# A two-block network on one core: the first half tile of attention's output weights split inside attention, the inputs of that projection split head by head, and small products around the barrier

## The chip, the cores and the metric

The kernel runs on one core of a Trainium2 chip. The metric is the device time of one execution in microseconds. The engines are TensorE (PE, with its weight loads as PEld), VectorE (DVE), ScalarE (ACT), GpSimd (POOL) and SyncE (SP, which here only issues DMAs).

## What is computed

Two networks of two layers each run one after the other on x of 256 tokens by 1024. The change lies in layer 0 of the first, windowed attention with a context of 256 further tokens, and its output projection with the residual and the layer norm:

```python
pz = h @ w_in
pzc = hc @ w_in
p, z = pz[..., :-E_WIDTH], pz[..., -E_WIDTH:]
pc, zc = pzc[..., :-E_WIDTH], pzc[..., -E_WIDTH:]
y, yc = attention_mixer(p, pc, attn_sink[j], row, col, not last)
x = layer_norm(alpha * x + gate * ((y * jax.nn.silu(z)) @ w_out[i]), ln_g[i], ln_b[i])
xc = layer_norm(alpha * xc + gate_c * ((yc * jax.nn.silu(zc)) @ w_out[i]), ln_g[i], ln_b[i])
```

Attention has 16 query heads of 128 (E_WIDTH is 2048) and 4 key heads; w_out[0] is 2048 x 1024. Layer 1 is an S5 mixer, and the second network has a gated-MLP and dilated attention layer, a gated linear attention layer and two convolutional feed-forward parts.

## The kernel before

**Phases.** The program is a row of phases: modulation, attention's input projection (qkvz), attention (`attention`, L807), its output projection (`residual_normalized`, L1033, with the names `out_...`), the S5 mixer (`ssm_...`), and so on. A phase is one block in which each engine has its own instruction list, written out by hand; semaphores order the engines against each other, and a barrier of all engines ends the block. Each engine reaches that barrier with a DRAIN, then POOL releases all. When more than 80 semaphores have been used up, a second barrier with a clearing of semaphores follows (L110, L111); this is so behind attention.

**Products in two parts.** The big products take f32 numbers as a sum of a lead and a rest: ACT copies a tile to the type fp32r (the lead), DVE subtracts the lead from the tile (the rest), and TensorE adds three products, lead by lead, lead by rest and rest by lead. `Split` (L215) does this for a weight that streams through a ring of two slots in SBUF (`core.ring`, 2 MB a slot). A weight tile of 1024 x 512 is split in two halves j = 0 and 1; `lead` (L266) and `rest` (L278) are one half, 128 partitions by 2048 elements, on ACT and on DVE. `start_scalar` (L287) and `start_vector` (L301) are the beginning of a phase: half 0, then the first piece of the other factor, then half 1, then its other pieces. With `src` given, as in the output projection, the other factor is split too, in pieces of four 128-row tiles (L299 the lead, L312 the rest). With `begun`, half 0 is taken as made before. `products` (L342) is TensorE's side: for each half it waits for the weights' rest and for the inputs' rest, and then goes through the token tiles t and the four rows k.

**Attention.** The loop runs `step(i)` for i from -1 to 17, on TensorE, ACT and DVE alike. In step i the scores of head i + 1, the turned outputs of head i - 2, the turned probabilities of head i, the turned queries of head i + 2 and the product with v of head i - 1 are made. The bank `ps_t` serves queries and outputs by turns. ACT's step is the copy to yzT (L964), the copy of the first probabilities (L968), the copy of the queries (L950) and the exponentials (L958, L959). DVE's step ends with the product of the output by z (L1016). POOL makes S5's input weights beside it, and SP carries them.

**Output projection.** n = 4 token tiles, two column groups of 512, and two ring tiles for each (the inner size is 2048). x is yzT, which holds one head in each of its 16 rows of tiles. POOL's work in this phase is `EarlyQuads` (L1487), ten pairs of small matrices for S5, six operations each (L1537, L1538, L1539), stored by SP (L1513); it begins when its tables (`ptab`, `cc`, L1506 and L1503) have landed and the first piece of x_rest is made:

```python
            def _(pool):
                pool.wait_ge(split.x_rest_made, 1)
                quads.make(pool)
```

SP's list issues the tables, the gate rows and the layer norm's rows, and the reloads of x and of the context first. The prefetch of S5's first weights stands before the last two pairs of POOL in SP's list. `spin(nc, bank, ident, n)` (L448) makes n products of ident by itself into a bank that nobody reads; 20 of them (L1077) stand at the end of this phase's TensorE list, and each product in the code is two records in the trace (L451 x40 for 20).

**Memory.** z, kn, q and v lie at the right end of SBUF (`within(heads, ...)`, L3478 on) and are given back behind attention.

Of the kernel before, what the change touches and what calls it, by code (L numbers as in the profile page):

```python
# [14 lines left out]
F32 = mybir.dt.float32  # L15
# [199 lines left out]
class Split:  # L215
# [6 lines left out]
    def __init__(self, core, ph, groups, halves, ntt, mm_done, src=None, lhs=None, slots=None, begun=False, flip=0):  # L222
        self.flip = flip
# [5 lines left out]
        if src is not None:  # L229
            lhs = [part("x_lead", [P, halves * KT, ntt * P]), part("x_rest", [P, halves * KT, ntt * P])]  # L230
# [53 lines left out]

    def _x_pieces(self):
        return range(2 * self.halves) if self.src is not None else ()

    def start_scalar(self, act, norm=None):

        for piece in range(2 * self.halves):  # L290
# [58 lines left out]
    def products(self, pe, bank, free, part_wait=None, between=None, unrolled=False, soon=None, after=None):  # L349
        nc, last_half = self.core.nc, 2 * self.halves - 1  # L350

        def group(g, parity):
            for sem, n in free:
                pe.wait_ge(sem, g * n + 1)
            for half in range(2 * self.halves):
                j = half % 2
                pe.wait_ge(self.rest_made, g * (2 * self.halves) + half + 1)
                if self.src is not None:
                    pe.wait_ge(self.x_rest_made, half + 1)
                for t in range(self.ntt):  # L360
                    for k in range(HK):
                        if part_wait is not None and t == 0 and g == 0:
# [24 lines left out]
class EarlyHalf:  # L387
# [419 lines left out]
def attention(core, q, kn, v, z, kT, work, yzT, xc):  # L807
# [7 lines left out]
    with phase(core, "attn") as ph:  # L815
# [22 lines left out]
        spare = ph.sb("spare", [P, DM])  # L838
        weights = InputWeights(core, ph, W_QKVZ, NWB - W_QKVZ, [core.x[:, s // 2, s % 2 * NW:(s % 2 + 1) * NW] for s in range(4)], [xc[:, s // 2, s % 2 * NW:(s % 2 + 1) * NW] for s in range(4)], [spare[:, s * NW:(s + 1) * NW] for s in range(2)])
# [5 lines left out]
        with ph.block() as block:  # L845
# [13 lines left out]
            def _(pe):  # L859
# [73 lines left out]
                for i in range(-1, NH + 2):  # L933
                    step(i, i % 2)

            @block.scalar
            def _(act):
# [37 lines left out]
                for i in range(-1, NH + 2):  # L975
                    step(i, i % 2)

# [2628 lines left out]
```

## Time and profile before

| | before |
|---|---|
| median of 3 runs (lowest to highest) | 1646.36 us (1642.62 to 1649.51) |
| the profiled execution: its time / its span | 1644.76 us / 1643.0 us |
| mean granted TensorE clock | 0.972 |
| PE / DVE / ACT / POOL busy | 94% / 60% / 48% / 40% |
| attention's last product to the first of out | 442.4 to 451.6 us |
| first product of out to S5's first | 451.6 to 546.4 us |

Times of rows are microseconds from the span's start. "Busy" of TensorE is modelled from the issue of its matmuls. The granted clock is a share of 2.4 GHz; 0.5 is 1.2 GHz.

### The profile page before, as it was taken

How to read it: one execution, taken by the hardware profiler on the slowest of the kernel's cores; microseconds unless marked ns; L12 is line 12 of the kernel's file. 1: busy time of each engine (PE TensorE's matmuls, PEld its weight loads, DVE VectorE, ACT ScalarE, POOL GpSimd, SP SyncE). 2: the span in 40 equal slices, each digit the busy share in tenths (PEclk: the TensorE clock that was granted, in tenths of full speed). 3: DMA queues.
4: the chain of work that ended last, by engine and by line, in shares of the span. 5: the costliest groups of instructions: out<-in, count | busy, mean ns of one | idle time of the engine just before them, and what ended most of it. 6: DMA issues, size and time to landing. Idle time of an engine off the chain costs nothing. (4 is left out here: it accounts for less than half of the span.)

```text
span 1643.0 us, 28520 instructions
## 1 busy us (share of the span) xinstructions
PE 1539.9 (94%) x11502; PEld 1321.2 (80%) x11502; DVE 981.9 (60%) x1349; ACT 794.7 (48%) x1075; POOL 649.5 (40%) x497
## 2 busy tenths in 40 slices
PE   4799999799699899999999999989999999999998
PEld 0488888588688688888889987778999877789997
DVE  6157722288654538757837546745766565557675
ACT  2532122355521576787564435645455364564552
POOL 0068989599699791749502106111000100210000
PEclk8899999999999999999989999989999999999999
DMA  9976877566452687988976455415453342264441
GB/s 387 426 265 213 273 239 249 167 194 193 149 207 95 218 253 207 258 250 259 231 244 236 167 189 198 154 52 210 182 224 153 132 157 111 103 231 184 201 163 42
DMA packets 120300, 331.32 MB, mean 202 GB/s; under 512 B 33509, under 2 KB 73189, under 8 KB 103929
## 3 DMA queue, kind: packets, MB, share of 16 engines
q1 hardware_dynamic: 117318, 304.20, 53.7%
q10 hardware_dynamic: 2868, 25.54, 4.3%
q8 instruction: 80, 1.31, 0.3%
q14 instruction: 34, 0.27, 0.1%
HBM read 283.48 MB, written 37.83 MB: 196 GB/s over the span
## 5 line engine op out<-in xcount | busy, mean ns | idle before, releaser
L3312 PE MATMUL ffn_ps<-ffn_x_lead,w_lead 128*128 128x256 f32 x672 | 188.4, 280 | 1.1 <-DVE w_rest L3391 1.1
L3312 PE MATMUL ffn_ps<-ffn_x_lead,w_rest 128*128 128x256 f32 x672 | 188.6, 281 | 0.0
L3312 PE MATMUL ffn_ps<-ffn_x_rest,w_lead 128*128 128x256 f32 x672 | 188.4, 280 | 0.0
L401 POOL TENSOR_TENSOR w_rest<-resident_ring,w_lead 128x2048 fp32r<-128x2048 f32 x7 | 32.1, 4590 | 387.9 <-ACT w_lead L397 200.3
L3391 DVE TENSOR_TENSOR w_rest<-resident_ring,w_lead 128x2048 fp32r<-128x2048 f32 x42 | 96.1, 2292 | 83.8 <-ACT w_lead L3356 83.8
L365 PE MATMUL qkvz_ps<-qkvz_w_lead,h_lead 128*128 128x512 f32 x320 | 125.8, 393 | 2.6 <-POOL h_rest L683 2.6
L3312 PEld LDWEIGHTS ffn_ps<-ffn_x_lead,w_lead 128*128 128x128 f32 x672 | 126.1, 188 | 2.1 <-issue 1.4
L3312 PEld LDWEIGHTS ffn_ps<-ffn_x_rest,w_lead 128*128 128x128 f32 x672 | 126.4, 188 | 0.7
L3312 PEld LDWEIGHTS ffn_ps<-ffn_x_lead,w_rest 128*128 128x128 f32 x672 | 126.3, 188 | 0.0
L365 PE MATMUL qkvz_ps<-qkvz_w_rest,h_lead 128*128 128x512 f32 x320 | 125.4, 392 | 0.0
L365 PE MATMUL qkvz_ps<-qkvz_w_lead,h_rest 128*128 128x512 f32 x320 | 125.2, 391 | 0.0
L282 DVE TENSOR_TENSOR w_rest<-resident_ring,w_lead 128x2048 fp32r<-128x2048 f32 x33 | 78.1, 2369 | 64.0 <-ACT w_lead L276 63.7
L276 ACT ACTIVATE qkvz_w_lead<-resident_ring 128x2048 fp32r<-128x2048 f32 x20 | 38.5, 1924 | 147.3 <-PE qkvz_ps L365 136.3
L282 DVE TENSOR_TENSOR qkvz_w_rest<-resident_ring,qkvz_w_lead 128x2048 fp32r<-128x2048 f32 x20 | 56.0, 2798 | 88.7 <-ACT qkvz_w_lead L276 88.7
L3356 ACT ACTIVATE w_lead<-resident_ring 128x2048 fp32r<-128x2048 f32 x42 | 80.1, 1912 | 50.7 <-PE ffn_ps L3312 50.6
L276 ACT ACTIVATE w_lead<-resident_ring 128x2048 fp32r<-128x2048 f32 x33 | 63.2, 1915 | 79.6 <-PE odd_ps L365 26.0
L1884 PE MATMUL ssm_ps_u<-h_lead,w_lead 128*128 128x512 f32 (+1 forms) x256 | 91.0, 355 | 6.8 <-DVE w_rest L2168 2.1
L1481 POOL TENSOR_TENSOR resident_x<-xc,resident_x 128x512 f32<-128x512 f32 x64 | 92.9, 1452 | 5.0
L2168 DVE TENSOR_TENSOR w_rest<-resident_ring,w_lead 128x1024 fp32r<-128x1024 f32 x32 | 48.9, 1530 | 68.8 <-ACT w_lead L2019 68.4
L1884 PE MATMUL ssm_ps_u<-h_lead,w_rest 128*128 128x512 f32 (+1 forms) x256 | 87.6, 342 | 1.4 <-issue 1.4
L1884 PE MATMUL ssm_ps_u<-h_rest,w_lead 128*128 128x512 f32 (+1 forms) x256 | 87.3, 341 | 0.0
L2318 PE MATMUL glu_ps<-h_lead,w_lead 128*128 128x256 f32 x256 | 71.7, 280 | 2.8 <-DVE w_rest L2358 1.5
(566 smaller groups left out, 4460.1 us busy)
## 6 DMA issues: line engine op xcount, KB each, us to landing
resident_ring<-in_ffn_gu SPq DMA_DIRECT2D x22, 2048.0 KB, 9.1
ffn_wd<-in_ffn_down SPq DMA_DIRECT2D x22, 1024.0 KB, 4.9
resident_ring<-in_ada_w SPq DMA_DIRECT2D x8, 2048.0 KB, 12.8
xc<-s_q_scratch SPq DMA_DIRECT2D x128, 128.0 KB, 3.3
resident_x<-in_s_bT SPq DMA_DIRECT2D x64, 256.0 KB, 3.8
resident_ring<-in_attn_w_in ACTq DMA_DIRECT2D x8, 2048.0 KB, 10.9
s_W_scratch<-resident_x SPq DMA_DIRECT2D x64, 256.0 KB, 2.7
resident_ring<-in_s_w SPq DMA_DIRECT2D x32, 512.0 KB, 6.0
```

Source lines behind the costliest of these rows:

```text
L276: self.core.nc.scalar.activation(self.w[0][j], self.core.tile(r)[:, j * HK:(j + 1) * HK, :], ACT.Copy).then_inc(self.lead_made, 1)
L282: self.core.nc.vector.tensor_tensor(self.w[1][j], self.core.tile(r)[:, j * HK:(j + 1) * HK, :], self.w[0][j].bitcast(F32), ALU.subtract).t ...
L365: last = nc.tensor.matmul(bank(parity, t), self.lhs[x][:, half * HK + k, t * P:(t + 1) * P], self.w[w][j][:, k, :], start=(half, k, x, w) ...
L401: self.core.nc.gpsimd.tensor_tensor(self.slots[1][0], self._raw(r), self.slots[0][0].bitcast(F32), ALU.subtract).then_inc(self.rest_made, 1)
L1481: g.tensor_tensor(b, q(0), b, ALU.mult).then_inc(self.scaled, 1)
L1884: last = nc.tensor.matmul(out, w[:, s, k, :], hparts[x][:, k, cols], start=k == 0 and x == 0 and w is w_lead, stop=k == KT - 1 and w is w_ ...
L2168: v.tensor_tensor(w_rest[:, u % 2], raw, w_lead[:, u % 2].bitcast(F32), ALU.subtract).then_inc(rest_made, 1)
L2318: last = nc.tensor.matmul(ps[s][:], w[s][:, k, :], parts[x][:, k, :], start=k == 0 and x == 0 and w is w_lead, stop=k == ET - 1 and w is w ...
L3312: last = nc.tensor.matmul(ps[s][f][:, m, :], w_part[w][m][:, k, f * P:(f + 1) * P], x_part[x][:, k, :], start=(k, w, x) == (0, 0, 0), stop ...
L3356: nc.scalar.activation(w_part[0][m], raw(s, m), ACT.Copy).then_inc(w_lead_made, 1)
L3391: v.tensor_tensor(w_part[1][m], raw(s, m), w_part[0][m].bitcast(F32), ALU.subtract).then_inc(w_rest_made, 1)
```

## The change

1. Half 0 of the first output weight tile is split inside attention: `EarlyHalf` takes the lead on ACT behind step 8 and the rest on DVE behind step 15. The parts lie where q lies (`w_parts`), in columns of heads that are done; the lead of yzT lies where z lies, kn takes the gate rows.
2. The first four heads of yzT are split one at a time (`fine_x`), and TensorE waits for each of them in its first token tile alone. POOL waits for four counts of `x_rest_made` in place of one, which now is the same four heads.
3. Small products: 12 at the end of attention's TensorE list, 10 at the start of the output projection's.

```diff
+    def x_parts_of(self, piece):
+        if self.fine_x and piece == 0:
+            return [(slice(k, k + 1), k + 1) for k in range(HK)]
+        return [(slice(piece * HK, (piece + 1) * HK), piece + (HK if self.fine_x else 1))]
...
             if self.src is not None:
-                ks = slice(piece * HK, (piece + 1) * HK)
-                self.core.nc.scalar.activation(self.lhs[0][:, ks], self.src[:, ks], ACT.Copy).then_inc(self.x_lead_made, 1)
+                for ks, count in self.x_parts_of(piece):
+                    self.core.nc.scalar.activation(self.lhs[0][:, ks], self.src[:, ks], ACT.Copy).then_inc(self.x_lead_made, 1)
...
             if self.src is not None:
-                ks = slice(piece * HK, (piece + 1) * HK)
-                dve.wait_ge(self.x_lead_made, piece + 1)
-                self.core.nc.vector.tensor_tensor(self.lhs[1][:, ks], self.src[:, ks], self.lhs[0][:, ks].bitcast(F32), ALU.subtract).then_inc(self.x_rest_made, 1)
+                for ks, count in self.x_parts_of(piece):
+                    dve.wait_ge(self.x_lead_made, count)
+                    self.core.nc.vector.tensor_tensor(self.lhs[1][:, ks], self.src[:, ks], self.lhs[0][:, ks].bitcast(F32), ALU.subtract).then_inc(self.x_rest_made, 1)
...
             for half in range(2 * self.halves):
                 j = half % 2
+                fine = self.fine_x and (g, half) == (0, 0)
                 pe.wait_ge(self.rest_made, g * (2 * self.halves) + half + 1)
-                if self.src is not None:
-                    pe.wait_ge(self.x_rest_made, half + 1)
+                if self.src is not None and not fine:
+                    pe.wait_ge(self.x_rest_made, self.x_parts_of(half)[-1][1])
                 for t in range(self.ntt):
                     for k in range(HK):
+                        if fine and t == 0:
+                            pe.wait_ge(self.x_rest_made, k + 1)
...
-    def rest(self, pool, r):
-        pool.wait_ge(self.lead_made, 1)
-        self.core.nc.gpsimd.tensor_tensor(self.slots[1][0], self._raw(r), self.slots[0][0].bitcast(F32), ALU.subtract).then_inc(self.rest_made, 1)
+    def rest(self, eng, r, ops=None):
+        eng.wait_ge(self.lead_made, 1)
+        (ops or self.core.nc.gpsimd).tensor_tensor(self.slots[1][0], self._raw(r), self.slots[0][0].bitcast(F32), ALU.subtract).then_inc(self.rest_made, 1)
...
+        following = EarlyHalf(core, ph, [[m] for m in first_weights])
+        FOLLOWING_AT = 8
...
                 for i in range(-1, NH + 2):
                     step(i, i % 2)
+                spin(nc, ps_s[0], ident, 12)
...
                 for i in range(-1, NH + 2):
                     step(i, i % 2)
+                    if i == FOLLOWING_AT:
+                        act.wait_ge(core.landed[0], 16 * (core.used[0] + 1))
+                        following.lead(act, 0)
...
                 for i in range(-1, NH + 2):
                     step(i, i % 2)
+                    if i == NH - 1:
+                        following.rest(dve, 0, nc.vector)
...
-        split = Split(core, ph, 2, 2, n, mm_done, src=yzT)
+        x_rest = ph.sb("x_rest", [P, ET, n * P], F32R)
+        split = Split(core, ph, 2, 2, n, mm_done, src=yzT, lhs=[x_lead, x_rest], slots=slots, begun=True, fine_x=True)
...
             def _(pool):
-                pool.wait_ge(split.x_rest_made, 1)
+                pool.wait_ge(split.x_rest_made, HK)
                 quads.make(pool)
...
             def _(pe):
+                spin(nc, ps[1][0], core.ident, 10)
                 split.products(pe, lambda s, t: ps[s][t][:], [])
...
+                    x_lead = nc.alloc_sbuf_tensor_at("out0_x_lead", [P, ET, NTOK], F32R, offset=nc.sbuf_top)
...
+                    w_parts = nc.alloc_sbuf_tensor_at("out0_w", [P, HK, 4, NW], F32R, offset=nc.sbuf_top)
+                    slots = [[w_parts[:, :, 2 * j + i, :] for j in range(2)] for i in range(2)]
...
-                                        again=((core.x[:], rows_of(d["x"])), (xc[:], rows_of(d["ctx"]))))
+                                        again=((core.x[:], rows_of(d["x"])), (xc[:], rows_of(d["ctx"]))),
+                                        x_lead=x_lead, slots=slots, gate=kn[:].rearrange("p t n -> p (t n)").rearrange("p (r n) -> p r n", r=2))
```

TensorE's list around the end of attention, before (the two branches are the end of one phase and the start of the next, with the barrier between them; names in square brackets are semaphores, called by the first owner of their number):

```order
L912 MATMUL attn_ps_t<-resident_ident,attn_yz 128x128 [waits attn_qT_ready,attn_yzT_ready,attn_yz_ready]
L912 MATMUL attn_ps_t<-resident_ident,attn_yz 128x128 x3
L845 UNCONDITIONAL_BRANCH
L1073 UNCONDITIONAL_BRANCH [waits barrier_Pool_Activation_PE_DVE_SP_release]
L365 MATMUL out_ps<-out_w_lead,out_x_lead 128x512 [waits ada_modT_done,ada_kept0]
```

and with the change:

```order
L923 MATMUL attn_ps_t<-resident_ident,attn_yz 128x128 [waits attn_qT_ready,attn_yzT_ready,attn_yz_ready]
L923 MATMUL attn_ps_t<-resident_ident,attn_yz 128x128 x3
L460 MATMUL attn_ps_s<-resident_ident 128x128 x12
L856 UNCONDITIONAL_BRANCH
L1090 UNCONDITIONAL_BRANCH [waits barrier_Pool_Activation_PE_DVE_SP_release]
L460 MATMUL out_ps<-resident_ident 128x128 x10
L374 MATMUL out_ps<-out_w,out_x_lead 128x512 [waits ada_modT_done,ada_kept0]
```

Twelve small products now stand ahead of the barrier and ten behind it; the first real product still waits for a weight rest and an input rest.

DVE's list at the same place, before:

```order
L1016 SCALAR_TENSOR_TENSOR attn_yz<-attn_ps_y,attn_rden,z 128x128 [waits attn_yz_turned,attn_pv_ready]
L845 UNCONDITIONAL_BRANCH
L1095 UNCONDITIONAL_BRANCH [waits barrier_Pool_Activation_PE_DVE_SP_release]
L282 TENSOR_TENSOR out_w_rest<-resident_ring,out_w_lead 128x2048 [waits ada_bias_made]
L312 TENSOR_TENSOR out_x_rest<-yzT,out_x_lead 128x2048 [waits ada_kept1]
```

and with the change:

```order
L410 TENSOR_TENSOR out_w<-resident_ring,out_w 128x4x512 [waits attn_early_lead_made]
L1031 SCALAR_TENSOR_TENSOR attn_yz<-attn_ps_y,attn_rden,z 128x128 [waits attn_yz_turned,attn_pv_ready]
L856 UNCONDITIONAL_BRANCH
L1113 UNCONDITIONAL_BRANCH [waits barrier_Pool_Activation_PE_DVE_SP_release]
L318 TENSOR_TENSOR out_x_rest<-yzT,out_x_lead 128x512 [waits ada_kept1] x4
L282 TENSOR_TENSOR out_w<-resident_ring,out_w 128x4x512 [waits ada_bias_made]
L318 TENSOR_TENSOR out_x_rest<-yzT,out_x_lead 128x2048 [waits ada_kept1] x3
```

The subtraction of half 0 moved ahead of the last product with z, and the first input piece became four. POOL's and SP's lists keep their order.

## Rows read from the trace of the kernel before

**Rows 1.** The page: busy time, share of the span and instructions of each engine.
```profile
PE 1539.9 (94%) x11502; PEld 1321.2 (80%) x11502; DVE 981.9 (60%) x1349; ACT 794.7 (48%) x1075; POOL 649.5 (40%) x497
```
**Rows 2.** Windows: us, busy (x) of PE, PEld, DVE, ACT, POOL; clock, DMA share, GB/s.
```profile
443.00:452.00 9.00, 0.46 (x2) 0.42 (x2) 5.03 (x3) 7.57 (x5) 0.46 (x1) 0.58 0.57 193
452.00:455.00 3.00, 3.00 (x9) 2.33 (x9) 3.00 (x2) 3.00 (x3) 3.00 (x2) 0.55 1.03 399
455.00:540.00 85.00, 85.00 (x377) 70.36 (x376) 41.77 (x39) 15.56 (x11) 82.10 (x56) 1.00 0.43 161
...
546.30:550.00 3.70, 3.03 (x24) 2.59 (x24) 2.13 (x3) 2.97 (x6) 1.31 (x2) 1.00 0.83 268
550.00:553.40 3.40, 2.49 (x13) 1.86 (x14) 3.31 (x7) 3.40 (x9) 1.16 (x2) 1.00 0.95 310
```
**Rows 3.** Timeline of TensorE: start, duration, what, count [idle before <-releaser].
```profile
442.41 0.66 PE L912 MATMUL attn_ps_t<-resident_ident,attn_yz 128*128 128x128 f32 x4 [1.22 <-DVE attn_yz L1016]
451.61 0.77 PE L365 MATMUL out_ps<-out_w_lead,out_x_lead 128*128 128x512 f32 x1 [8.54 <-DVE out_x_rest L312]
...
454.71 0.39 PE L365 MATMUL out_ps<-out_w_rest,out_x_lead 128*128 128x512 f32 x1
```
**Rows 4.** Timeline of DVE and ACT around the barrier.
```profile
441.23 1.13 DVE L1016 SCALAR_TENSOR_TENSOR attn_yz<-attn_ps_y,attn_rden,z 128x128 f32<-128x128 f32 x4 [3.43 <-PE attn_ps_y L903]
...
445.03 1.91 ACT L276 ACTIVATE out_w_lead<-resident_ring 128x2048 fp32r<-128x2048 f32 x1 [1.33 <-PEq L111]
...
449.18 2.28 DVE L312 TENSOR_TENSOR out_x_rest<-yzT,out_x_lead 128x2048 fp32r<-128x2048 f32 x1
451.38 2.28 DVE L282 TENSOR_TENSOR out_w_rest<-resident_ring,out_w_lead 128x2048 fp32r<-128x2048 f32 x1
```
**Rows 5.** Timeline of POOL in out, and its window over the phase.
```profile
451.54 3.10 POOL L1537 TENSOR_TENSOR out_vp_v<-out_vp_ptab,out_vp_cc 128x512 f32<-128x512 f32 x1 [14.68 <-DVE out_x_rest L312]
454.60 3.15 POOL L1538 TENSOR_TENSOR out_vp_tmp<-out_vp_ptab,out_vp_cc 128x512 f32<-128x512 f32 x1
...
481.46 1.11 POOL L1537 TENSOR_TENSOR out_vp_v<-out_vp_ptab,out_vp_cc 128x512 f32<-128x512 f32 x1
...
542.42 1.27 POOL L1539 TENSOR_TENSOR out_vp_v<-out_vp_v,out_vp_tmp 128x512 f32<-128x512 f32 x1
451.50:543.70 92.20, 89.09 (x60) 0.98 0.47 176
```
**Rows 6.** SP's issue of cc; DMA issues (KB, us to landing), 425:545, then 444.9:450.
```profile
445.38 0.90 SPq L1503 DMA_DIRECT2D out_vp_cc<-in_s_cA  x2
...
s_V_scratch<-out_vp_v SPq DMA_DIRECT2D x20, 256.0 KB, 2.2
...
out_vp_cc<-in_s_cA SPq DMA_DIRECT2D x2, 128.0 KB, 4.5
```
**Rows 7.** The barrier lines L845 and L1051: duration ns, start; and the small products.
```profile
L845 PEldq DRAIN  x1: 700/700/700, 442.4 to 442.4; - x1
L845 ACTq DRAIN  x1: 627/627/627, 443.1 to 443.1; - x1
L1051 PEldq DRAIN  x1: 2173/2173/2173, 542.7 to 542.7; - x1
L1051 ACTq DRAIN  x1: 1907/1907/1907, 543.6 to 543.6; - x1
L1051 SPq DRAIN  x1: 7/7/7, 546.1 to 546.1; - x1
540.19 4.63 PE L451 MATMUL out_ps<-resident_ident 128*128 128x128 f32 x40
```
**Rows 8.** Timeline of ACT and TensorE at the change from step 8 to 9.
```profile
388.72 0.60 ACT L964 ACTIVATE yzT<-attn_ps_t 128x512 f32<-128x512 f32 x1 [1.02 <-PE attn_ps_t L912]
389.83 0.60 PE L871 MATMUL attn_ps_t<-resident_ident,q 128*128 128x128 f32 x4
```
**Rows 9.** One line of DVE in S5's start: a subtraction of 128x512.
```profile
L673 DVE TENSOR_TENSOR h_rest<-ssm_ps_s,h_lead x2: 690/690/691, 551.1 to 555.7; 128x512 fp32r<-128x512 f32 x2
```

More of the change, by code:

```diff
@@ L215, with __init__ @@
 class Split:
-    def __init__(self, core, ph, groups, halves, ntt, mm_done, src=None, lhs=None, slots=None, begun=False, flip=0):
-        self.flip = flip
+    def __init__(self, core, ph, groups, halves, ntt, mm_done, src=None, lhs=None, slots=None, begun=False, flip=0, fine_x=False):
+        self.flip, self.fine_x = flip, fine_x
         self.core, self.groups, self.halves, self.ntt, self.mm_done, self.src = core, groups, halves, ntt, mm_done, src
@@ L228, in __init__ @@
         self.w, self.begun = slots, begun
-        if src is not None:
+        if src is not None and lhs is None:
             lhs = [part("x_lead", [P, halves * KT, ntt * P]), part("x_rest", [P, halves * KT, ntt * P])]
@@ L804, in _, with attention @@
                     dve.sem_inc(dve_free, LT)
-def attention(core, q, kn, v, z, kT, work, yzT, xc):
+def attention(core, q, kn, v, z, kT, work, yzT, xc, first_weights):
     nc, d = core.nc, core.d
@@ L1030, in residual_rows, with residual_normalized @@
     return 16 * (len(rows) + len(more))
-def residual_normalized(core, name, weights, xs, yzT, following, again):
+def residual_normalized(core, name, weights, xs, yzT, following, again, x_lead, slots, gate):
     nc, d = core.nc, core.d
@@ L1038, in residual_normalized @@
     with phase(core, name) as ph:
-        gate = ph.sb("gate", [P, 2, DM])
         ln_g, ln_b = ph.sb("ln_g", [P, KT]), ph.sb("ln_b", [P, KT])
@@ L3458, in build @@
                 context = [(xc[:, t, :], 1) for t in range(LT)]
-                with ExitStack() as heads, ExitStack() as outputs:
+                with ExitStack() as heads, ExitStack() as values, ExitStack() as outputs:
                     z = within(heads, "z", [P, TT, E], side="right")
+                    x_lead = nc.alloc_sbuf_tensor_at("out0_x_lead", [P, ET, NTOK], F32R, offset=nc.sbuf_top)
                     kn = within(heads, "kn", [P, TT, KVW], side="right")
@@ L3464, in build @@
                     q = within(heads, "q", [P, TT, E], side="right")
-                    v = within(heads, "v", [P, TT, KVW], side="right")
+                    w_parts = nc.alloc_sbuf_tensor_at("out0_w", [P, HK, 4, NW], F32R, offset=nc.sbuf_top)
+                    slots = [[w_parts[:, :, 2 * j + i, :] for j in range(2)] for i in range(2)]
+                    v = within(values, "v", [P, TT, KVW], side="right")
                     with ExitStack() as inner:
@@ L3471, in build @@
                         kT, work = within(inner, "kT", [P, KVH, NTOK]), within(inner, "work", [P, KT - 1, NTOK])
-                        attention(core, q, kn, v, z, kT, work, yzT, xc)
-                    heads.close()
+                        attention(core, q, kn, v, z, kT, work, yzT, xc, [of[0] for of in slots])
+                    values.close()
                     rows_of = lambda m: m.rearrange("(t p) n -> p t n", p=P)
                     residual_normalized(core, "out0", "w_out0", latent + context, yzT, lambda sp: s5_prefetch(core, sp),
-                                        again=((core.x[:], rows_of(d["x"])), (xc[:], rows_of(d["ctx"]))))
+                                        again=((core.x[:], rows_of(d["x"])), (xc[:], rows_of(d["ctx"]))),
+                                        x_lead=x_lead, slots=slots, gate=kn[:].rearrange("p t n -> p (t n)").rearrange("p (r n) -> p r n", r=2))
                 wparts = [within(ctx, n, [P, HK * NW], F32R, side="right") for n in ("w0_lead", "w0_rest")]
```

## Prediction

> **What bounds the kernel now.** I read the page first. TensorE is busy 94% of the span [rows 1], so the question is where it is not busy or not fast, and which of those places this change touches. The chain that ended last reaches back only to the last feed-forward part, far behind the edit, so it says nothing here. The windows by stage do [rows 2]: from 443 to 452 us TensorE does 0.46 us of work at a mean granted clock of 0.58. After that, from 455 to 540, it is busy all the time at 1.00. The hole lies between attention and the output projection ("out"). The timeline of TensorE shows both sides [rows 3]: its last transposes of attention start at 442.41, the first product of out at 451.61. The products that start from 451.61 to 454.71 are seven in 3.10 us; at the later pace, 377 products in 85.0 us [rows 2], or 0.226 us each, they would take 1.6. So the low clock (1.2 GHz, fallen while TensorE idled) costs 1.5 us, and the wait itself 8.5.
>
> What fills the wait is in the rows of ACT and DVE [rows 4]: after the barrier ACT copies half a weight tile (1.91 us from 445.03) and then a piece of yzT. DVE subtracts after each, and its first piece of x_rest ends at 449.18 + 2.28 = 451.46, when TensorE starts.
>
> The same semaphore starts POOL, and the end of the phase has to be read from there. POOL makes S5's matrices from 451.54 and ends its last operation at 542.42 + 1.27 = 543.69, with no pause to speak of: sixty operations in 92 us [rows 5]. SP stores the last one (landing 2.2 us after issue in the median [rows 6]) and reaches the closing barrier at 546.1 [rows 7]. ACT is there at 543.6 + 1.91 = 545.5, TensorE at 542.7 + 2.17 = 544.8. **The phase ends when POOL's chain and its last store do**; TensorE's own path has 0.6 us of slack already. A gain ahead of the products counts only as far as POOL starts earlier too.
>
> **The change, part by part.**
>
> *Half tile split inside attention.* ACT gets 1.91 us [rows 4] behind the exponentials of step 8. The ACT queue is idle 1.02 us there before the copy to yzT at 388.72 [rows 8]; that copy starts about 0.8 late and ends at 390.1, and TensorE's transposes of q, at 389.83 now, need its bank. TensorE never pauses in these steps, so about +0.3 us stays. DVE's 2.28 us goes ahead of its last product with z, at 441.23, before which it idles 3.43 us [rows 4]: free. If that cover were gone, attention's end would move by what sticks out of it. POOL, which such a subtraction holds up (below), has ended its attention work by then (idle 14.68 us before 451.54, so from 436.9 [rows 5]).
>
> *Twelve small products before the barrier.* Forty records of the same 128x128 product take 4.63 us behind out [rows 7], 0.116 each, and each one in the code is two records. Twelve are 2.8 us, from 442.85 to 445.65. Does the barrier wait for them? The drain of TensorE's queue at the end of out begins at 542.7 and takes 2.17 us, to 544.8, exactly where those 40 records end, and in attention it ends with the last transposes (442.4 + 0.70) [rows 7]. So it does wait. ACT's drain, the last one now, ends at 443.1 + 0.63 = 443.7 [rows 7]. The barrier moves from there to 445.7, **+2.0 us**, with SP, DVE, POOL and ACT held behind it. The Trainium skill (Perfetto Trace Analysis, section "Per-engine timelines", on sequencer-only instructions such as DRAIN) draws a DRAIN with only the sequencer and the semaphore in it; by that the small products would not hold the barrier and this term would be 0. The 2.17 us row speaks against it, and the row decides.
>
> Out then starts at 445.03 + 0.3 + 2.0 = 447.3.
>
> *Ten small products behind the barrier, inputs head by head.* The ten take 20 x 0.116 = 2.3 us: to 449.6. The first head needs one ACT copy of 128x512 (0.60 [rows 8]) and one DVE subtraction of that shape (0.69 [rows 9]): 448.6, so the small products, not the data, set the start. Later heads come every 0.6 to 0.7 us, and TensorE uses three products (0.68) for each. The second half of the tile follows 10.9 us later, its parts are made by about 456: covered. With TensorE busy on both sides of a gap of some 1.5 us I take the clock as staying at 2.4 GHz, since in the window from 546.3 it is 1.00 behind such a gap [rows 2]. TensorE gains 451.6 - 449.6 = 2.0 plus the 1.5: **3.5 us**; its last product ends near 536.7, ACT's last normalization near 542.0.
>
> *POOL.* It waits for four heads (447.3 + 0.6 + 4 x 0.65 = 450.5) but also for its tables: the first DMA for cc is issued at 445.38, 0.4 us into the phase, and lands 4.5 us later [rows 6], so at 452.2. Before, they were 1.7 us ahead of need; now they are last. What does 0.7 us of lateness cost? While DVE subtracts in SBUF, a POOL operation of 1.11 us takes 3.10 or 3.15 [rows 5]: the first one starts at 451.54, DVE's subtraction from 451.38 ends at 453.66, and POOL ends at 454.64. With the change ACT has four short copies (2.0) and one lead (1.9) before that subtraction: it starts at 451.3 again and ends at 453.6, and POOL's first operation, though later, ends near 454.6 as before. So **0** for POOL's chain, with 546.3 as the phase's end again. The Trainium skill (SBUF — State Buffer, section "Who interferes with whom") says that the one which starts first holds the pair for the whole instruction, and that the other blocks. Were it a sharing of bandwidth, the phase would end 0.7 later. The trace agrees with the first.
>
> Bounds of this term: if the barrier is not held, the second weight subtraction and with it POOL come 2.0 earlier: -2.0. If the lateness counts in full: +0.7.
>
> *What is late next.* TensorE ends its 20 small products at 541.3 and then idles 5 us instead of 1.6. No row has an idle time of that length: 1.6 us leaves the clock at 1.00, 8.5 lets it fall [rows 2]. I take it as falling. In rows 3 it cost 1.5 us, and S5's start has 0.7 us of idle time in its first 3.7 us [rows 2] that takes up some: **+0.9**. Bounds: 0, and with all of 546.3 to 553.4 at half clock 5.5 us of busy time more, less 1.6 idle: +3.9.
>
> The other edits cost nothing: the gate rows land in kn instead of a tile of their own, the same two DMAs; the weight parts are strided by 4 x 512 over 2048 elements, the same element count.
>
> Sum: +0.9 on the profiled execution's own 1644.76, so 1645.7. That execution is 1.6 us under the median of the three runs (1646.36); 0.9 on the median gives 1647.3. I say **1646.5 us**. Differences under 0.5% (8.2 us) can't be told from none in this kernel.
>
> **The rivals.**
>
> *Faster, the barrier is not held or POOL does start earlier.* For it: the barrier's own wait is short, and the small products write banks that nobody waits for. Against it: the 2.17 us drain. POOL's end moves by -2.0, and S5's start costs less: 1646.5 - 2.0 - 0.9, near 1643.6. Chance 0.17. Were POOL no bound at all, the 3.5 and the 2.0 would both arrive: 1641. Chance 0.03.
>
> *Slower, the clock at S5's start.* One mechanism: the longer idle time before 546.4. It decides if the clock is still at 1.2 GHz once S5's first transposes are over and its products begin. Price up to +3.9 in place of 0.9: 1649.5, and 1650.5 with the 0.7. For it: every part of 3.5 us gained before is idle time there. Against it: the start is full of waits for ACT and POOL. The Trainium skill (TensorE: Matmul & The Clock Gate, Part 1) calls the throttled state the default that activity releases; that is this case. Chance 0.15.
>
> *The change does not do what it says:* the gaps of 1.2 us between attention's last products are enough for the clock to fall at 444 as now [rows 2, 3]; then the small products run at half pace, the barrier comes another 1.2 later, POOL's chain with it: 1647.7. Chance 0.08.
>
> **How the numbers follow.** The forecast has 0.57. No case reaches 8.2 us: the best is 5.5 under the forecast, the worst 4 over. The three runs of one kernel lie within 6.9 us, though, and such scatter puts a few per cent on either side: faster by over 0.5% 0.04, within 0.5% 0.91, slower 0.05. The range, 1642 to 1650.5, holds the forecast with its scatter and nearly all of two rivals, and leaves out the last 0.03.
>
> **What would show it.** Right: TensorE's drain ends attention near 445.7 and the phase starts near 447.3; ten small products at 1.00, first product near 449.6; POOL's first operation near 452 and long; POOL's end near 543.7, S5 near 546.4 with a clock under 1. Wrong: a phase start near 445.4, POOL's last operation before 542, or an S5 that starts at full clock after a shorter gap.

## The result, and the profile after

| | before | changed |
|---|---|---|
| median, side by side on one chip | 1644.11 us (20 runs, 1638.9 to 1650.6) | 1652.29 us (20 runs, 1645.47 to 1656.48) |
| ratio, 95% interval | | 1.005 (1.0038 to 1.0062) |
| profiled execution, span | 1643.0 us | 1654.3 us |

The ratio is that of the fast runs and need not be the quotient of the two medians; with its interval it decides here and below.

The changed kernel is 8.2 us slower. The forecast was 1646.5 us in a range up to 1650.5, so the result lies outside the range, on the slower side.

First the place that the prediction was about. The barrier behind attention in the changed kernel: duration of the drains in ns and their start.
```profile
L856 ACTq DRAIN  x1: 626/626/626, 444.2 to 444.2; - x1
L856 PEldq DRAIN  x1: 2173/2173/2173, 444.7 to 444.7; - x1
L856 SPq EVENT_SEMAPHORE  x1: 17/17/17, 447.0 to 447.0; - x1
```
TensorE's drain takes 2.17 us where it took 0.70 [rows 7] and ends at 446.8, when the small products do. ACT's ended at 444.8. So the small products hold the barrier by 2.0 us, the size predicted. Then the timeline of TensorE, POOL and the windows of the phase:
```profile
443.97 2.84 PE L460 MATMUL attn_ps_s<-resident_ident 128*128 128x128 f32 x24
448.16 2.47 PE L460 MATMUL out_ps<-resident_ident 128*128 128x128 f32 x20 [1.35 <-PEq L111]
450.39 0.72 PE L374 MATMUL out_ps<-out_w,out_x_lead 128*128 128x512 f32 x2
```
```profile
453.71 1.81 POOL L1555 TENSOR_TENSOR out_vp_v<-out_vp_ptab,out_vp_cc 128x512 f32<-128x512 f32 x1 [16.61 <-DMA out_vp_cc<-in_s_cA]
...
543.56 1.27 POOL L1557 TENSOR_TENSOR out_vp_v<-out_vp_v,out_vp_tmp 128x512 f32<-128x512 f32 x1
```
```profile
443.00:452.00 9.00, 7.17 (x55) 6.75 (x56) 2.92 (x6) 4.39 (x6) 0.00 (x0) 1.00 0.31 96
...
547.10:550.50 3.40, 2.26 (x11) 2.29 (x12) 1.13 (x3) 1.16 (x2) 0.58 (x1) 0.57 0.48 193
```
The clock stays at 1.00 across the barrier (0.58 in [rows 2]), the first product of out starts 2.3 us after the phase does, POOL waits for the cc transfer, and the clock is low when S5 starts. All that was foreseen. The phase of out ends at 548.1, against 546.3 before: 1.8 us late.

The loss is behind it. I compare the lengths of the phases, each from one release of the barrier to the next in the two traces. The span grew by 11.3 us, 3.1 us more than the medians: the profiled execution of the changed kernel (1656.04 us) is 3.8 us above its median, that of before (1644.76) 0.7. **S5 +11.05** (301.55 to 312.60), attention +3.39 (138.85 to 142.24), output projection -1.27 (101.35 to 100.08), modulation +1.00, input projection -1.28, S5's gate +0.57, the dilated attention layer of the second network -1.94, all the others together -0.2. The change edits nothing in S5. Windows over exactly S5, before and changed (length, busy us of PE, PEld, DVE, ACT, POOL, then clock, DMA share, GB/s):
```profile
546.30:847.90 301.60, 283.84 (x4028) 250.98 (x4028) 191.20 (x297) 211.54 (x298) 178.11 (x138) 0.95 0.81 232
```
```profile
548.10:860.80 312.70, 290.96 (x4028) 256.33 (x4028) 190.58 (x297) 210.68 (x298) 178.28 (x138) 0.93 0.78 222
```
The same 4028 products, on an engine that is busy 7.1 us longer (the clock is low more of the time, 42.9 us in place of 27.3) and idle 4.0 us longer. What TensorE's idle time in S5 ended with, of the kind that no semaphore explains ("issue"), before and then changed:
```profile
PE ssm_ps_u L1884 <- issue: 2.6, 2, 1.4
PE ssm_ps_y L1937 <- issue: 0.9, 1, 0.9
```
```profile
PE ssm_ps_y L1955 <- issue: 6.7, 4, 2.0
PE ssm_ps_s L2006 <- issue: 1.8, 1, 1.8
PE ssm_ps_u L1902 <- issue: 1.5, 2, 1.2
PE ssm_ps_l L1937 <- issue: 1.1, 1, 1.1
```
3.5 us have become 11.1. One pause of 1.18 us near 570 is in every kernel below; without it 2.3 have become 9.9, in two pauses before and seven now. Such a pause looks like this in the timeline, and beside it stands the DMA of the 1.1 us from 666.8:
```profile
669.23 0.31 PE L1955 MATMUL ssm_ps_y<-ssm_V,ssm_hs 128*32 128x128 f32 x3 [1.89 <-issue]
```
```profile
q1 hardware_dynamic: 108, 0.18, 44.0%
q8 instruction: 1, 0.02, 5.4%
```
A packet on the queue "instruction" ran from 666.90 to 667.86, and TensorE went on 1.4 us after its end. Each of the nine pauses ends 1.3 to 1.6 us after the end of such a packet (the one near 570 doesn't: 14 and 25 us). The page of the changed kernel says how large these are:
```profile
q8 instruction: 80, 1.31, 0.3%
```
80 packets, 1.31 MB: 16 KB each. PE's compiled list has 20,592 instructions before, and 80 packets of 256 instructions make 20,480, so that a packet brings about 256 of them. The Trainium skill has the same number (Advanced Engine Details and Errata, section "ISA Cache": a line is 16 KB or 256 instructions). The trace agrees.

The change adds 22 small products, each of four instructions of TensorE: 88. (The page of before counts 28,520 instructions, that of the kernel with these products alone, spins_only below, 28,608.) Everything behind them lies 88 places later in the list, and so the point at which a new packet is needed falls on another product of S5.

**Theory A**: where the packets' borders fall in S5 costs the time; the change merely shifts them. **Theory B**: the change's own work (spins, drain, clock) leaves S5 slower. "Place" below is by how many instructions of TensorE S5 stands later than before. A small product is called a spin.

### The profile page after: what moved, and what is told of

Read it like the earlier page. It is cut to its first block and busy times, and to the rows that moved or that the text cites. A ratio compares the mean times of both kernels' runs of the same rounds, so it can differ in the third digit from the quotient of the medians.

```text
span 1654.3 us, 28616 instructions
## 1 busy us (share of the span) xinstructions
PE 1556.6 (94%) x11546; PEld 1332.0 (81%) x11546; DVE 982.2 (59%) x1352; ACT 794.4 (48%) x1078; POOL 646.0 (39%) x497
## 3 DMA queue, kind: packets, MB, share of 16 engines
q8 instruction: 80, 1.31, 0.3%
## 5 line engine op out<-in xcount | busy, mean ns | idle before, releaser
L1499 POOL TENSOR_TENSOR resident_x<-xc,resident_x 128x512 f32<-128x512 f32 x64 | 87.1, 1362 | 5.0
L374 PE MATMUL out_ps<-out_w,out_x_lead 128*128 128x512 f32 x256 | 80.3, 395 | 0.0
## 6 DMA issues: line engine op xcount, KB each, us to landing
resident_ring<-in_attn_w_in ACTq DMA_DIRECT2D x8, 2048.0 KB, 10.2
```

Source lines behind the costliest of these rows:

```text
L374: last = nc.tensor.matmul(bank(parity, t), self.lhs[x][:, half * HK + k, t * P:(t + 1) * P], self.w[w][j][:, k, :], start=(half, k, x, w) ...
L1499: g.tensor_tensor(b, q(0), b, ALU.mult).then_inc(self.scaled, 1)
```

## The experiments

### First four: the place alone, and the change without its small products

pad88 and pad128 are the kernel before with an unused semaphore's increments at the head of TensorE's list, after_pad168 is the changed kernel with such increments (88 + 168 = 256), and no_spins is the changed kernel with the early half tile and the fine inputs but no spins (place 0).

```diff
 # pad88, at the start of the modulation's list of TensorE (128, 168 in the others)
+                for _ in range(88):
+                    pe.sem_inc(pad, 1)
```
```diff
 # no_spins
-                spin(nc, ps_s[0], ident, 12)
...
-                spin(nc, ps[1][0], core.ident, 10)
```

> The kernel before with nothing of the change, but 88 semaphore increments on TensorE's list at the very start of the program, where TensorE idles until 10.7 us. They make TensorE's list exactly as much longer as the change does (20680 instructions in place of 20592), so every later instruction of TensorE stands where it stands with the change. Theory A (the S5 phase got slower because TensorE's instructions arrive later at some places, which depends on where they stand in the list): barrier to barrier S5 takes 306 to 313 us in place of 301.6, with pauses of TensorE of 1 to 2 us that no semaphore explains, and the time is 4 to 9 us over the kernel before. Theory B (S5 got slower because it starts after a longer idle time, at a low clock and with shifted transfers): nothing changes, S5 within 2 us of 301.6 and the time within 1.5 us.

> The kernel before with 128 semaphore increments at the start of TensorE's list, half a fetch. Theory A: S5 differs from 301.6 by some microseconds, either way, by where the boundaries of the fetches fall; I expect +2 to +9. Theory B: no change, within 1.5 us.

> The changed kernel with 168 semaphore increments at the start of TensorE's list: with the change's 88 they make 256 instructions, the size of one fetch of TensorE's instructions (16 KB, 64 bytes each), so that each later instruction stands at the same place within a fetch as before the change. Theory A: S5 takes 301 to 304 us, and the time is 1 to 3 us over the kernel before (attention +3.4, out -1.3 as in the changed kernel's trace). Theory B: S5 stays at 306 to 313 us and the time at +8.

> The changed kernel without its 12 and 10 small products; the split inside attention and the head-by-head inputs stay. TensorE's list is as long as before the change (20592). The barrier is no longer held by TensorE. Theory A: S5 within 2 us of 301.6, attention's phase 139 to 140.5 (from 138.9), out's first product about 2 us behind the phase's start, at 1.2 GHz; POOL's chain starts 1 to 2 us earlier than before the change; time between -3 and 0 against the kernel before. Theory B: the idle time before S5 is still there (TensorE's path is ahead of POOL's by more than before), so S5 is 4 to 9 us longer and the time +3 to +7.

Measured, against 1643.18 us of before in the same comparison: pad88 1655.03 (ratio 1.0061, 1.0041 to 1.008), pad128 1653.2 (1.005, 1.0032 to 1.0068), after_pad168 1651.58 (1.0045, 1.0029 to 1.006), no_spins 1641.4 (0.9984, 0.9969 to 0.9998). S5 took 312.51, 308.45, 298.36 and 301.52 us. Each length of a phase, here and below, is that of one profiled execution. Window and waits of S5 in pad88:
```profile
550.10:862.60 312.50, 292.56 (x4028) 258.74 (x4028) 189.05 (x297) 211.19 (x298) 178.04 (x138) 0.93 0.78 223
```
```profile
PE ssm_ps_y L1940 <- issue: 3.8, 3, 2.3
PE ssm_ps_u L1887 <- issue: 3.3, 2, 2.1
PE ssm_ps_s L1991 <- issue: 2.0, 1, 2.0
```
88 instructions that compute nothing make S5 of the kernel *before* 11 us longer, as in the changed one (312.60). Its total is above what I expected (+10.0 us by the ratio, against +4 to +9). By its total, after_pad168 is a miss for theory A (+7.4 against +1 to +3), but its S5 is back and shorter than expected (301 to 304); the modulation took 84.72 us in place of 74.48, since the increments stand in front of TensorE's first product. That 10.2 us is the padding's own price. It also mixes into pad88 (2.5 us) and pad128 (4.0), so the padding had to be hidden. Both figures are rough, since in the seven kernels of this study without padding in the modulation it takes 74.3 to 76.8 us.

### Padding where TensorE waits anyway, and the parts of the change

TensorE waits 23.8 us for weights in the modulation, over 8 waits. The padding goes in front of the waits behind the first one, which alone takes 10.7 us; 13.1 us are left to hide it in.

```diff
 # spread88 (before, 11 each), after_spread168 (changed, 21 each), spread256 (before, 32 each)
                 def unit(g):
+                    if 1 <= g <= 8:
+                        for _ in range(11):
+                            pe.sem_inc(pad, 1)
```
```diff
 # spins_only: the kernel before, with
+                spin(nc, ps_s[0], ident, 12)
...
+                spin(nc, ps[1][0], core.ident, 10)
```
```diff
 # late_spins: the changed kernel, without
-                spin(nc, ps_s[0], ident, 12)
```

> The kernel before plus 88 increments of an unused semaphore in PE's list, 11 in front of each of the weight waits of units 1 to 8 of the modulation, where PE waits for DMA anyway (23.8 us over 8 waits). It is pad88 without the price of the increments. Theory A (where PE's later instructions lie, modulo 256 of the 64-byte instructions that one fetch brings, sets how often PE stands without a wait in S5): the modulation stays at 74.5 to 75.5 us (pad88: 76.99), S5 takes 309 to 314 us as in pad88 (312.51) and in the changed kernel (312.60), total +8 to +11 us. Theory P (pad88's loss was the price of its own increments): S5 stays at 301.5, total within +-2 us.

> The changed kernel plus 168 increments of an unused semaphore, 21 in front of each of the weight waits of units 1 to 8 of the modulation. With the change's 88 PE instructions, PE's list behind them stands 256 instructions later than before, so its fetch boundaries fall where they fell. Theory A: the modulation takes 75 to 77 us (after_pad168: 84.72, the increments in front of the first wait cost it 10), S5 takes 298 to 303 us (changed kernel 312.60, after_pad168 298.36), attention stays at +3.4 us, the output projection at -1.3 to -2, total 1643 to 1646 us, 0 to +2 against before. Theory B (the spins and the drain themselves leave S5 slower): S5 stays at 309 to 313 and the total at +8.

> The kernel before with the two rows of spins alone, 12 in front of the barrier behind attention and 10 behind it; no early half tile, no fine inputs. Theory A with the drain: PE's drain at attention's end waits for the spins, attention +2 to +3 us; the 10 spins stand beside the 8.5 us in which PE waits for the first inputs, output projection 101 to 101.5; S5 309 to 314; total +10 to +13 us. Theory B' (the early half, not the spins, costs attention its 3.4 us): attention within 0.5 us of before, total +8 to +10.

> The changed kernel without the 12 spins in front of the barrier (48 PE instructions fewer, so its list stands 40 instructions later than before, not 88); the 10 spins behind the barrier stay. Drain theory: attention falls from 142.2 us to 139.2 to 140.2 (no_spins 139.23), ACT or POOL end the barrier again; the output projection takes 99.5 to 100.5. Theory A: S5 takes another length, that of a place between 0 (301.5) and 88 (312.5): 300 to 313 us. Total 1640 to 1650 us. Rival: the 12 spins cost nothing in front of the barrier and attention stays at 142.

Measured, before 1642.95: spread88 1653.53 (1.0061, 1.004 to 1.0082), **after_spread168 1641.8 (0.9996, 0.9981 to 1.0012)**, spins_only 1650.88 (1.0043, 1.0026 to 1.006), late_spins 1642.7 (1.0006, 0.999 to 1.0023). The changed kernel with 168 idle instructions more is as fast as before: its loss of 8.2 us is gone, though all spins, the held barrier and the early half tile are still in it. That is a little better than expected (0 to +2 us, S5 298 to 303). spread88 comes out as theory A has it, but for 0.5 us more in the modulation (76.03). The S5 of spread88, the term alone, and then that of after_spread168, each with its pauses:
```profile
548.60:859.40 310.80, 290.68 (x4028) 256.44 (x4028) 190.04 (x297) 211.13 (x298) 178.21 (x138) 0.93 0.78 225
```
```profile
PE ssm_ps_y L1941 <- issue: 3.5, 3, 2.0
PE ssm_ps_u L1888 <- issue: 2.8, 2, 1.6
PE ssm_ps_s L1992 <- issue: 1.1, 1, 1.1
PE ssm_ps_l L1923 <- issue: 0.5, 1, 0.5
```
```profile
546.90:843.40 296.50, 282.12 (x4028) 249.33 (x4028) 190.31 (x297) 211.74 (x298) 178.26 (x138) 0.96 0.82 236
```
```profile
PE ssm_ps_y L1959 <- issue: 1.5, 1, 1.5
PE ssm_ps_u L1906 <- issue: 1.4, 2, 1.2
PE ssm_ps_s L1978 <- issue: 1.2, 1, 1.2
```
Theory B falls. Late_spins' S5, at place 40, took 299.22 us (just below the 300 to 313 expected), so that not every shift costs. spins_only has the long S5 (309.59), but its total is +7.1 us where I expected +10 to +13: its S5 is 8.0 us longer, at the lower end of what I expected. The drain comes out as predicted: attention takes +2.2 us with the spins alone (141.02) and +0.4 with the early half alone (139.29 in late_spins, 139.23 in no_spins). The barrier in spins_only and in late_spins:
```profile
L845 ACTq DRAIN  x1: 626/626/626, 443.5 to 443.5; - x1
L845 PEldq DRAIN  x1: 2173/2173/2173, 444.0 to 444.0; - x1
```
```profile
L856 PEldq DRAIN  x1: 700/700/700, 444.3 to 444.3; - x1
L856 ACTq DRAIN  x1: 627/627/627, 445.0 to 445.0; - x1
```

### Is it the number, or the number modulo 256? Does it need S5 behind it?

```diff
 # behind88: the kernel before, in S5's gate phase, right behind S5
             @block.tensor
             def _(pe):
+                for _ in range(88):
+                    pe.sem_inc(pad, 1)
```
```diff
 # no_spins_no_fine, on no_spins
-        split = Split(core, ph, 2, 2, n, mm_done, src=yzT, lhs=[x_lead, x_rest], slots=slots, begun=True, fine_x=True)
+        split = Split(core, ph, 2, 2, n, mm_done, src=yzT, lhs=[x_lead, x_rest], slots=slots, begun=True)
...
-                pool.wait_ge(split.x_rest_made, HK)
+                pool.wait_ge(split.x_rest_made, 1)
```
no_spins_spread256 is no_spins with the 8 x 32 increments.

> The kernel before plus 256 increments of an unused semaphore, 32 in front of each of the weight waits of units 1 to 8 of the modulation: nearly three times the increments of spread88 (+10.6 us), but a whole fetch block of 256 instructions. Theory A (place modulo 256): S5 as before or as in after_spread168, 296 to 302 us, the increments cost the modulation 0 to 3 us, total -3 to +2 us. Theory N (more instructions in PE's list, whatever their number, cost S5 time): S5 309 or more, total at least +10 us.

> The kernel before plus 88 increments of an unused semaphore at the start of PE's list in the phase behind S5 (the gate). It is the control of spread88: the same number of instructions, but S5 stands in front of them. Theory A: S5 stays at 301.5 us, the gate phase takes 0 to 2.5 us more for the increments, the phases behind it move by less than 1 us each, total 0 to +4 us. Theory N (any 88 more instructions in PE's list, wherever they stand): total +8 us or more.

> The changed kernel without its 22 spins (early half tile and fine inputs stay), plus 256 increments spread over units 1 to 8 of the modulation. It is the version that the runs so far point to: no_spins gave 0.9984, and the two kernels that stand 256 instructions later had the shortest S5 (298.36 and 296.40 us against 301.5 at 0). If that gain is of the place (an absolute place, not only modulo 256), S5 takes 296 to 299 us and the total is 1636 to 1640 us; if the place counts modulo 256 alone and those two were scatter, S5 takes 301 to 302 and the total is that of no_spins, 1640 to 1643 us.

> no_spins with the first inputs in one piece again instead of head by head: what is left of the change is the early half tile. PE's first product comes when the whole first piece is subtracted, about 2.5 us later after the phase's start than in no_spins (1.65 us). If the output projection ends with POOL's chain and the landing of its last transfer (in no_spins SP's wait ends 544.65, ACT's drain 543.55, a slack of 1.1 to 1.4 us), the phase takes 99.8 to 101.2 us (no_spins 99.80, before 101.35), total 0 to +1.5 us over no_spins, 1641 to 1643. Rival: each microsecond of PE's start counts, phase 102 or more.

Measured, before 1642.04: spread256 1646.06 (1.0025, 1.001 to 1.0041), behind88 1657.32 (1.0098, 1.0078 to 1.0119), no_spins_spread256 1646.49 (1.0027, 1.0012 to 1.0042), no_spins_no_fine 1641.31 (1.0005, 0.9993 to 1.0016).

With 256 instructions S5 takes 298.93 us, with 88 it took 310.83: not the number, the place. (The unused semaphore is in both, so it isn't that either. The pages of all five kernels at place 256 count 81 packets of 16 KB, those of the others 80.) The total of spread256 still missed what I expected by 2 us, since the modulation took 80.10 (+5.6 us). behind88 shows why. S5 in front of its padding is as before (300.36 us), which is theory A's part; but the gate phase took 110.52 us in place of 95.44, and its waits and the increments read:
```profile
PE glu_ps L2321 <- issue: 14.8, 1, 14.8
```
```profile
L2310 PEldq EVENT_SEMAPHORE  x88: 51/51/51, 850.7 to 864.0; - x88
```
88 increments in 13.3 us are 0.15 us each, five times what I had worked out from pad88 (2.5 us / 88). There most of the increments lay beside the first wait: TensorE's first product starts at 14.40 us in pad88 and at 10.69 in before. The total of behind88, +16 us, meets what its expectation wrote down for theory N (+8 or more) and misses theory A's 0 to +4. But 15.1 us of it lie in the gate phase, where the increments stand, and S5 is not longer: it is the padding's price, and no evidence for N.

no_spins_spread256 paid 8.0 us in the modulation (82.32, no_spins 74.29) and had an S5 of 298.99, 2.5 us shorter; the total had to miss what I expected by the price of the padding. In no_spins_no_fine the first product comes 4.5 us after the phase's start (1.65 in no_spins) and the output projection takes 101.73 us in place of 99.80. Its barrier:
```profile
L1067 ACTq DRAIN  x1: 1906/1906/1906, 547.1 to 547.1; - x1
L1067 SPq DRAIN  x1: 7/7/7, 547.6 to 547.6; - x1
```
ACT ends it, at 549.0, 1.4 us after SP: TensorE's own path, which ACT's last normalization follows, is the last again. TensorE's last product starts 96.0 us after the phase's start, against 92.8 in no_spins. So the fine inputs earn about 1.9 us of the phase in these profiles, more than the 1.5 us I took as the upper end. In the totals the two can't be told apart for certain: 1.0005 and 0.9984, with intervals that overlap.

### Two candidates, padded with products

So far the size of the place's effect was mixed with the price of the increments. Two last kernels pad no_spins with spins.
```diff
 # no_spins_spun64 (8 in front of units 1 to 8; no_spins_spun10: 2 in front of units 1 to 5)
                         pe.wait_ge(kept_done[g % 2], g // 2)
+                    if 1 <= g <= 8:
+                        spin(nc, ps[g % 2], core.ident, 8)
```

> no_spins plus 64 products of the unit matrix with itself in the modulation, 8 in front of each of the weight waits of units 1 to 8: 256 PE instructions, a whole fetch block, by products in place of semaphore increments. 64 products take 64 x 0.12 to 0.23 us = 7.4 to 15 us, beside 24 us of waits for weights. Theory A: S5 takes 296 to 301 us as in the four kernels that stand 256 later (298.36, 296.40, 298.93, 299.00), the modulation 74.3 to 77, total 1637 to 1642 us. Rival (a price of the modulation, a falling S5 only by increments): total 1643 or more.

> no_spins plus 10 products of the unit matrix in the modulation, 2 in front of the weight waits of units 1 to 5: PE's list stands 40 instructions later than in no_spins, the place of late_spins, whose S5 took 299.22 us. Theory A: S5 298 to 301 us, the modulation 74.3 to 76, total 1638 to 1642 us. Rival (the place says nothing, late_spins' S5 was scatter): S5 301.5, total that of no_spins, 1640 to 1643.

Measured, before 1642.71: no_spins_spun64 1640.13 (0.9984, 0.9971 to 0.9997), no_spins_spun10 1641.71 (0.9999, 0.9984 to 1.0014). S5 300.46 and 296.16 us. Padding with products acts like padding with increments, and is cheap (modulation 75.8 and 76.3 us). The S5 of no_spins_spun10 is below what I expected (298 to 301), yet its total doesn't differ for certain from that of no_spins. no_spins_spun64 and no_spins, both 0.16% under before, are the fastest kernels of the study; both beat the changed kernel clearly and before only barely. Neither shows a gain over no_spins in the total. S5 by place, over all profiled executions (the column of pauses leaves out the one near 570):

| place | kernels | S5, us | pauses behind a packet, sum, us | at the low clock, us |
|---|---|---|---|---|
| 0 | before, no_spins, no_spins_no_fine, behind88 | 300.4 to 301.6 | 2.3 to 3.9 | 27.3 to 30.7 |
| 40 | late_spins, no_spins_spun10 | 299.2, 296.2 | 3.1, 1.7 | 23.9, 20.5 |
| 88 | changed, pad88, spread88, spins_only | 309.6 to 312.6 | 6.8 to 9.9 | 37.5 to 46.3 |
| 128 | pad128 | 308.5 | 9.7 | 27.3 |
| 256 | after_pad168, after_spread168, spread256, no_spins_spread256, no_spins_spun64 | 296.4 to 300.5 | 2.5 to 5.3 | 20.5 to 26.4 |

In all five kernels at 88 and 128 S5 takes at least 6.9 us longer than in any of the eleven others and has more of these pauses, whatever else is in them. The smaller differences, of places 40 and 256 against 0, are not shown by the totals: late_spins and no_spins_spun10 have 1.0006 and 0.9999, no_spins with its longer S5 has 0.9984.

## Why the prediction was wrong

*Where it failed.* The sum priced each edit at the place where it stands and ended with "no case reaches 8.2 us". It counted the 22 spins as 2.8 and 2.3 us of TensorE, and not as 88 instructions in front of everything that follows. The trace of before had the sign of it, in the two pauses shown above that end with no semaphore, and no rival asked what they were. The missing term is +8 to +11 us in S5 (place 88 against before), shown by spread88, which has the term alone (+9.3 in S5, total 1.0061), and by after_spread168, which has everything else (total 0.9996).

*Half tile in attention, +0.3.* Right: +0.4 in late_spins and no_spins. The changed kernel's own trace has attention at +3.4, 1.0 more than 2.0 and 0.4 make. This 1.0 us comes in the first 5 us of the phase and with the clock: 10.2 us of attention are at the low clock there, 6.8 in before, and pad88, which changes nothing in attention, has the same 10.2 and +1.05. spins_only (+2.2) and after_spread168 (+2.5) have 6.8, as before.

*Spins hold the barrier, +2.0.* Right: 2.03 between ACT's drain and TensorE's in the trace, +2.2 in spins_only. The Trainium skill's picture of a DRAIN as work of the sequencer alone (Perfetto Trace Analysis, section "Per-engine timelines") would have given 0; four rows of 2173 ns against 700 ns decide against reading it so.

*TensorE gains 3.5.* Right: its spins behind out start at 539.78, before at 540.19, while the phase began 3.1 us later: 3.5 us gained. The spins have a part in it, but only as a pair. TensorE's last product of out starts 95.0 us after the phase's start in before, 92.8 in no_spins, 91.5 in the changed kernel and 94.4 in late_spins: the half tile and the fine inputs give 2.2 us, both rows of spins 1.3 more, and the ten behind the barrier without the twelve ahead of it take 1.6 away, since TensorE reaches them with a fallen clock (0.50 from 446.8 to 451.2 in late_spins, where the ten take 4.61 us in place of 2.47). The phase shows little of that (99.80 in no_spins, 100.08 in the changed kernel, 100.05 in late_spins): in the first two POOL's chain and its last store end it, in late_spins TensorE's path does.

*POOL's chain, 0, the phase's end again at 546.3.* The mechanism was right: cc lands last, and POOL's first operation ends 7.5 us after the phase's start (9.7 before, 7.3 forecast). That its lateness costs nothing is borne out: in the eight kernels with the half tile and the fine inputs this operation starts 5.14 to 5.66 us after the phase's start and ends at 7.45 to 7.47 in each, 1.0 after DVE's subtraction (6.48 in the changed kernel). The chain ends 96.8 us after the start, 2.0 less than before (98.8). The size of the last step was off: the last store lands 2.86 us after its issue, before 2.16, so the phase won 1.3 and not 2.3. That is scatter of the store, which lands after 2.0 to 3.6 us in the 16 profiles; in after_spread168, with 2.15, the phase takes 99.35 us and has won 2.0.

*S5's start, +0.9.* Right in its mechanism (clock 0.57 in the window from 547.1), and small: ACT's first copy behind the start comes 0.46 us later than before. The slower rival put a low clock here at up to 3.9; that is not where the 11 us are. The sum of that rival has a slip (1649.5 and 0.7 are 1650.2, not 1650.5), which changes nothing here.

*"Can't be told from none."* The prediction set this at 0.5% (8.2 us). The measured difference is just that large, and 20 runs of each kernel tell it clearly: the interval is 1.0038 to 1.0062.

*What the change itself is worth.* after_spread168 against before: 0.9996 (0.9981 to 1.0012), -0.7 us. S5 was some 2.5 us shorter at place 256 than at 0 in the mean of the profiles, so the rest may be up to +2 or so; the prediction's +0.9 fits. The 12 spins in front of the barrier, +2.0, are the costliest of its parts in the traces; without any spins the change is worth -2.6 us (0.9984, 0.9969 to 0.9998, so barely clear of none).

**Open.** The S5 difference between before and changed splits into longer pauses (2.3 to 9.9 us, of which 3.6 come back in waits on other engines that get shorter) and into products at the low clock (busy time +7.1). The second need not follow from the first: pad128 has pauses as long as the changed kernel's and no more low clock than before. Why a border costs 2 us on one product and nothing on another was not tried: no run moved a border by single instructions. In the changed kernel packets follow each other as closely as 4.1 us (815.3 and 819.4) in this part of S5, so that short products without waits may use up a packet before the next is there; this is argued, not shown. A count over the 16 profiles fits it. Of the 21 packets in S5 that start 450 or more records of TensorE (products and weight loads) after the packet before, 16 have such a pause behind them; of the 300 that start after fewer than 300 records, 9 have one. Whether the late packets are late because the DMA queues are busy was not tried. That the pattern repeats each 256 rests on one period.

## What to carry to other kernels

Before pricing an edit that adds or removes instructions on the busiest engine, list its idle time that ends with no semaphore and set it against the packets of the instruction queue: where there are such pauses, an edit ahead of them can move the time by the shift alone (here 0.6% for 88 idle instructions), and such a difference says nothing about the edit. Test that by shifting the list: hide a block of idle instructions in a long wait, once to the same place as the changed kernel without the change, and once with the change to a full block of 256. And work that only keeps an engine warm must end before the barrier's last other engine does, since the drain waits for it.

## What I had not expected of the hardware

- 88 instructions that compute nothing, in the first phase, make one that starts 470 us later 9 to 11 us longer (spread88 310.8, pad88 312.5, before 301.6 us); 256 of them do not (298.9).
- A pause of TensorE ends 1.0 to 1.6 us after the end of a 16 KB packet of instructions, in all 16 profiles; the packet itself took about 1.0 us.
- A semaphore increment in TensorE's list costs 0.15 us (88 in 13.3 us), its record shows 51 ns of it. The four instructions of a small product take 0.23 us (20 products, 40 records, in 4.63 us), less than two increments.
- TensorE's drain lasts until its products are done: 2173 ns behind spins, 700 ns behind transposes.
